# A ring of five raw slots, seven in the expert stage, with five high and four low split slots, and ScalarE's order around small turns

## Reference

```python
def swiglu(h, w_gate, w_up, w_down):
    return (jax.nn.silu(h @ w_gate) * (h @ w_up)) @ w_down

def moe_swiglu(h, w_router, b_router, w1, w3, w2):      # shortened
    top_val, top_idx = lax.top_k((xt @ w_router + b_router), 2)
    gates = jax.nn.softmax(top_val, axis=-1)
    ...                                                 # rows sorted by expert, in blocks
    def run_block(args):
        tok, e = args
        xb = x_pad[tok]
        hb = jax.nn.silu(xb @ w1[e]) * (xb @ w3[e])
        return hb @ w2[e]
    ...                                                 # each row times its gate, added to its token

def reference(x, c, ...):
    for l in range(2):
        sh_m, sc_m, g_m, sh_f, sc_f, g_f = split(silu(c) @ ada_w[l] + ada_b[l])
        h = rms_norm(x, norm_mix_pre[l]) * (1 + sc_m) + sh_m
        x = x + g_m * rms_norm(hybrid_mixer(h, ...), norm_mix_post[l])
        h = rms_norm(x, norm_ffn_pre[l]) * (1 + sc_f) + sh_f
        y = swiglu(h, ...) if l == 0 else moe_swiglu(h, ...)
        x = x + g_f * rms_norm(y, norm_ffn_post[l])
```

## Time and profile before

| | |
|---|---|
| time, median of 3 | 1459.69 us (1458.56 to 1461.4) |
| profiled execution | 1459.97 us; its span 1458.2 us |
| granted TensorE clock | 0.997 |
| PE busy | 1427.9 us, 98% |
| VectorE busy | 1278.9 us, 88% |
| ScalarE busy | 1022.2 us, 70% |
| moved by DMA | 506.88 MB, mean 348 GB/s |

### The profile page before, as it was taken

How to read it: one execution, slowest core, us unless ns; L and a number is a source line. 1 busy time by engine, 2 the same in 40 slices (tenths; PEclk the granted TensorE clock), 3 DMA queues, 4 the chain that set the end, 5 groups by cost and what they waited for, 6 DMA issues and landing times.

```text
span 1458.2 us, 18907 instructions
## 1 busy us (share of the span) xinstructions
PE 1427.9 (98%) x7352; PEld 1205.8 (83%) x7352; DVE 1278.9 (88%) x1263; ACT 1022.2 (70%) x992; POOL 81.5 (6%) x109
## 2 busy tenths in 40 slices
PE   9999999999999999999999999999999999999996
PEld 5799889878889988888888878788788788888885
DVE  6899888977777768999999989999998999999995
ACT  2774454434576358778888889888879888888874
POOL 5000000000000000000000002000000010000010
PEclk9999999999999999999999999999999999999998
DMA  9849859987554855999999999999999999999993
GB/s 371 342 181 355 311 180 387 388 346 268 184 195 145 287 219 211 374 414 367 406 422 421 420 377 399 409 421 420 418 418 408 409 414 420 420 409 420 421 409 116
DMA packets 74274, 506.88 MB, mean 348 GB/s; under 512 B 8385, under 2 KB 8513, under 8 KB 16706
## 3 DMA queue, kind: packets, MB, share of 16 engines
q1 hardware_dynamic: 69986, 490.91, 83.9%
q0 software_dynamic: 4192, 14.70, 3.4%
HBM read 498.74 MB, written 6.83 MB: 347 GB/s over the span
## 4 chain that ended last, share of the span: by engine, by line
PE 63%; issue 18%; DVE 14%; ACT 3%; DMA 1%; POOL 1%; SPq 0%; DVEq 0%; ACTq 0%; POOLq 0%
PE ps L1936 17%; PE ps L1938 16%; PE ps L1937 16%; DVE lo L1237 10%; PE ps L1997 2%; PE ps L2424 2%; PE ps L2425 2%; PE ps L2461 2%; ACT hi L698 2%; DMA gate_m<-rows_x,gather_row 1%; PE ps L2161 1%; PE ps L2144 1%; ACT hi L682 1%; DVE lo L1208 1%; DVE bT_lo L1767 1%
## 5 line engine op out<-in xcount | busy, mean ns | idle before, releaser
L1237 DVE TENSOR_TENSOR lo<-raw,hi 128x2048 fp32r<-128x2048 f32 x336 | 755.8, 2286 | 48.9 <-ACT hi L698 47.7
L698 ACT ACTIVATE hi<-raw 128x2048 fp32r<-128x2048 f32 x336 | 637.6, 1920 | 86.2 <-PE ps L1938 60.4
L1936 PE MATMUL ps<-hi,hT_hi 128*128 128x512 f32 (+3 forms) x896 | 348.2, 389 | 4.1 <-DVE hT_lo L1264 1.9
L1938 PE MATMUL ps<-hi,hT_lo 128*128 128x512 f32 (+3 forms) x896 | 342.5, 382 | 0.0
L1937 PE MATMUL ps<-lo,hT_hi 128*128 128x512 f32 (+3 forms) x896 | 342.2, 382 | 0.0
L1208 DVE TENSOR_TENSOR lo<-raw,hi 128x2048 fp32r<-128x2048 f32 (+3 forms) x83 | 176.9, 2145 | 37.6 <-ACT hi L682 36.2
L1936 PEld LDWEIGHTS ps<-hi,hT_hi 128*128 128x128 f32 x896 | 168.3, 188 | 38.7 <-issue 4.3
L1938 PEld LDWEIGHTS ps<-hi,hT_lo 128*128 128x128 f32 x896 | 168.2, 188 | 32.0
L1937 PEld LDWEIGHTS ps<-lo,hT_hi 128*128 128x128 f32 x896 | 168.4, 188 | 30.0 <-issue 0.2
L682 ACT ACTIVATE hi<-raw 128x2048 fp32r<-128x2048 f32 (+3 forms) x83 | 147.2, 1798 | 34.3 <-DMA raw<-in_w_fg_dram 15.2
L1936 PE MATMUL ps<-hi,bT_hi 128*128 128x512 f32 (+1 forms) x408 | 160.5, 393 | 7.2 <-DVE bT_lo L1767 7.1
(11 more groups left out here) (348 smaller groups left out, 1638.1 us busy)
## 6 DMA issues: line engine op xcount, KB each, us to landing
raw<-in_moe_w_dram SPq DMA_DIRECT2D x336, 1024.0 KB, 8.9
raw<-in_w_ada_dram SPq DMA_DIRECT2D x40, 1024.0 KB, 6.4
raw<-in_w_fd_dram SPq DMA_DIRECT2D x11, 1024.0 KB, 7.1
raw<-in_w_ga_dram SPq DMA_DIRECT2D x8, 1024.0 KB, 5.6
raw<-in_w_gb_dram SPq DMA_DIRECT2D x8, 1024.0 KB, 5.2
raw<-in_w_ab_dram SPq DMA_DIRECT2D x8, 1024.0 KB, 5.1
raw<-in_w_o_dram SPq DMA_DIRECT2D x8, 1024.0 KB, 6.9
raw<-in_w_fg_dram SPq DMA_DIRECT2D x8, 1024.0 KB, 6.7
```

The source lines that it names most:

```text
L698: act.activation(hi[:, (s - PLAIN) % NSPLIT, :], raw[:, r % NRAW, :], ACT.Copy).then_inc(hi_done, 1)
L1237: dve.tensor_tensor(lo[:, at, :], raw[:, r % NRAW, :], hi[:, at, :].bitcast(f32), ALU.subtract).then_inc(raw_done, 1)
L1936: pe.matmul(o, wh, mh, start=first, stop=False)
L1938: return pe.matmul(o, wl, mh, start=False, stop=last)
```

## The change

- `NSPLIT` = 4 becomes five `hi` slots (`NHIGH`) and four `lo` slots (`NLOW`). VectorE's `lo` now waits itself for `used` of the chunk four before; ScalarE's `hi` for the one five before.
- `NRAW` goes from 6 to 5. `raw_ring` works out for each load its slot and the load that had it before. From expert chunk 5 (`JOIN`) to chunk 319 (`LEAVE` is 320) two more slots are in the ring, both in r6. Their first loads wait for the zero rows (`rows_out`) and the normed rows (`xn_out`) to be written out.
- Small items' weighted rows go to `gate_m` instead of r6. For that a gather into `gate_m` waits for the scatter before it, and `weighted_y` of a small item for the turn of the next small item's rows. The last load of the result into r6 waits for the last chunk in the slot there.
- After a small unit, ScalarE makes `hi` of b+4 and b+5 first, then `small_silu`, then the silu or copy of w1, then `small_hi`.

The diff, cut to its core (elsewhere `raw[:, r % NRAW, ...]`, `hi[...]` and `lo[...]` are replaced by the helpers shown):

```diff
@@ -51,7 +51,9 @@
 SPARE = 3
 ITEMS = EXPERTS + SPARE
 CH = 2048
-NRAW, NSPLIT = 6, 4
+NRAW, NHIGH, NLOW = 5, 5, 4
+EXTRA = 2
+JOIN, LEAVE = 5, 320
 PER_ITEM = 6 * NG
 EPS = 1e-6
 NEG = -1.0e30
@@ -145,6 +147,29 @@
 STREAM = stream()
 RAW_OF = {(kind, n, q): r for r, (kind, n, q) in enumerate(STREAM)}
 NR = len(STREAM)
+
+
+def raw_ring():
+
+    out, free, fills, last = [], list(range(NRAW)), [0] * (NRAW + EXTRA), [None] * (NRAW + EXTRA)
+    for r in range(NR + ITEMS * PER_ITEM):
+        c = r - NR
+        if c == JOIN:
+            free = list(range(NRAW, NRAW + EXTRA)) + free
+        slot = free.pop(0)
+        if not (slot >= NRAW and c >= LEAVE):
+            free.append(slot)
+        else:
+            slot = free.pop(0)
+            free.append(slot)
+        fills[slot] += 1
+        out.append((slot, fills[slot], last[slot]))
+        last[slot] = r
+    return out
+
+
+RING = raw_ring()
+LAST_IN = [max(r for r, (s, _, _) in enumerate(RING) if s == slot) for slot in range(NRAW + EXTRA)]
 
 
 GATES = [(l, v) for l, v in ADA if v in (G_M, G_F)]
@@ -254,8 +279,8 @@
 
 
         raw = sb("raw", [P, NRAW, CH])
-        hi = sb("hi", [P, NSPLIT, CH], f32r)
-        lo = sb("lo", [P, NSPLIT, CH], f32r)
+        hi = sb("hi", [P, NHIGH, CH], f32r)
+        lo = sb("lo", [P, NLOW, CH], f32r)
         x = sb("x_tok", [P, T, D])
         r2 = sb("r2", [P, T * D])
         r3 = sb("r3", [P, T * D])
@@ -350,7 +375,7 @@
         x_rows_of = {False: cbc, True: gate_m}
         x_staged = {False: r3[:, 0:K * P].rearrange("p (k s) -> p k s", k=K),
                     True: r3[:, 1536:1536 + K * HALF_CAP].rearrange("p (k s) -> p k s", k=K)}
-        y_rows = {False: r5[:, :], True: r6[:, 0:D]}
+        y_rows = {False: r5[:, :], True: gate_m[:, :]}
 
         def x_pair(i):
 
@@ -368,6 +393,19 @@
         def large_slots(n):
             return slice(4, 8) if n == UNITS_ALL - 1 else slice(0, 4)
 
+        def raw_of(r, e=CH):
+            slot = RING[r][0]
+            return raw[:, slot, 0:e] if slot < NRAW else r6[:, (slot - NRAW) * CH:(slot - NRAW) * CH + e]
+
+        def high_of(s, e=CH):
+            return hi[:, (s - PLAIN) % NHIGH, 0:e]
+
+        def low_of(s, e=CH):
+            return lo[:, (s - PLAIN) % NLOW, 0:e]
+
+        def wait_full(engine, r):
+            engine.wait_ge(raw_full[RING[r][0]], 16 * RING[r][1])
+
         def h_at(m):
             return 4 + 8 * (m - 1) if m else 0
 
@@ -448,7 +486,13 @@
 
             def slot_free(r):
 
-                sp.wait_ge(raw_done, r + 1)
+                slot, fill, before_ = RING[r]
+                if before_ is not None:
+                    sp.wait_ge(raw_done, before_ + 1)
+                elif slot == NRAW:
+                    sp.wait_ge(rows_out, 16)
+                elif slot == NRAW + 1:
+                    sp.wait_ge(xn_out, 16)
 
             def early_load(s):
                 _, t, (a, b), _ = WEIGHTS[s]
@@ -478,16 +521,16 @@
                 else:
                     _, t, (a, b), e = WEIGHTS[n]
                     src = A[t][a, b]
-                sp.dma_start(raw[:, r % NRAW, 0:e], src).then_inc(raw_full[r % NRAW], 16)
+                sp.dma_start(raw_of(r, e), src).then_inc(raw_full[RING[r][0]], 16)
                 if kind == "first":
                     early_load(q)
 
             def moe_load(r, kind, e, g, half):
-                slot_free(r - NRAW)
+                slot_free(r)
                 src = A["moe_" + kind]
                 src = src[e, g, half] if isinstance(e, int) else \
                     src[bass.ds(e, 1), g, half, :, :].rearrange("e p n -> p (e n)")
-                sp.dma_start(raw[:, r % NRAW, :], src).then_inc(raw_full[r % NRAW], 16)
+                sp.dma_start(raw_of(r), src).then_inc(raw_full[RING[r][0]], 16)
 
             expert = {0: 0}
 
@@ -666,6 +711,7 @@
                 if n in FINISH_AT:
                     scatter_rows(FINISH_AT[n])
             pool.wait_ge(rows_out, ALL_ROWS)
+            pool.wait_ge(raw_done, LAST_IN[NRAW] + 1)
             pool.dma_start(y_exp, rows_y[0:SEQ].rearrange("(t p) d -> p t d", p=P)).then_inc(y_in, 16)
 
 
@@ -676,10 +722,10 @@
             def hi_part(s):
                 r = RAW_OF["w", s, 0]
                 e = WEIGHTS[s][3]
-                act.wait_ge(raw_full[r % NRAW], 16 * (r // NRAW + 1))
-                if s >= PLAIN + NSPLIT:
-                    act.wait_ge(used, s - NSPLIT + 1)
-                act.activation(hi[:, (s - PLAIN) % NSPLIT, 0:e], raw[:, r % NRAW, 0:e], ACT.Copy).then_inc(hi_done, 1)
+                wait_full(act, r)
+                if s >= PLAIN + NHIGH:
+                    act.wait_ge(used, s - NHIGH + 1)
+                act.activation(high_of(s, e), raw_of(r, e), ACT.Copy).then_inc(hi_done, 1)
 
             def upto(name, ahead=2):
 
@@ -1009,7 +1055,10 @@
 
                 small, before_ = i >= LARGE, same_kind_before(FINISH, i)
                 act.wait_ge(used, NW + unit_chunk(FINAL[i], "w2", 1) + 1)
-                act.wait_ge(rows_out, 16 if before_ is None else ROWS_OUT[before_])
+                if before_ is not None:
+                    act.wait_ge(rows_out, ROWS_OUT[before_])
+                if small and i + 1 < EXPERTS:
+                    act.wait_ge(m_gath, 2 * PREP_OF[i + 1] + 2)
                 bank = 6 if small else 4
                 act.activation(y_rows[small].rearrange("p (c s) -> p c s", c=2), ps[:, bank:bank + 2, :], ACT.Identity,
                                scale=held[:, i, 2:3]).then_inc(m_yc, 1)
@@ -1025,18 +1074,21 @@
                 if n in FINISH_AT:
                     weighted_y(FINISH_AT[n])
                 moe_hi(b + 3)
-                if n:
+                if n and SMALL[n - 1]:
+                    moe_hi(b + 4, b + 5)
+                    small_silu(n - 1)
+                elif n:
                     moe_hi(b + 4)
-                    (small_silu if SMALL[n - 1] else hidden_hi)(n - 1)
+                    hidden_hi(n - 1)
                     moe_hi(b + 5)
-                    if SMALL[n - 1]:
-                        small_hi(n - 1)
                 after = b + 6 if n else 4
                 up_done(n, "w1")
                 if SMALL[n]:
                     act.activation(gate_s, ps[:, 0, :], ACT.Copy).then_inc(m_silu, 1)
                 else:
                     act.activation(h_large, ps[:, 0, :], ACT.Silu).then_inc(m_silu, 1)
+                if n and SMALL[n - 1]:
+                    small_hi(n - 1)
                 if (i, g) == (END, 3):
                     act.wait_ge(m_gt, 1)
                     act.activation(r4[:, 512:512 + SEQ], ps[:, 3, 0:SEQ], ACT.Copy).then_inc(m_gtc, 1)
@@ -1141,9 +1193,9 @@
 
                 l, v = ADA[a]
                 r = RAW_OF["ada", a, q]
-                dve.wait_ge(raw_full[r % NRAW], 16 * (r // NRAW + 1))
+                wait_full(dve, r)
                 for kk in range(2):
-                    w = raw[:, r % NRAW, kk * D:(kk + 1) * D]
+                    w = raw_of(r)[:, kk * D:(kk + 1) * D]
                     k = 2 * q + kk
                     m = dve.scalar_tensor_tensor(w, w, 1.0, cbc[:, :], ALU.mult, ALU.mult, accum_out=av[:, k:k + 1])
                 m.then_inc(raw_done, 1)
@@ -1940,7 +1991,7 @@
             def chunk(name):
                 s = CHUNK[name]
                 pe.wait_ge(raw_done, RAW_OF["w", s, 0] + 1)
-                return hi[:, (s - PLAIN) % NSPLIT, :], lo[:, (s - PLAIN) % NSPLIT, :]
+                return high_of(s), low_of(s)
 
             def finish(name, m):
                 m.then_inc(used, 1)
```

More of the change, by code:

```diff
@@ L390, in build @@
         x_rooted = sem("x_rooted")
-        raw_full = [sem(f"raw_full{i}") for i in range(NRAW)]
+        raw_full = [sem(f"raw_full{i}") for i in range(NRAW + EXTRA)]
         early_in = [sem(f"early_in{s}") for s in range(PLAIN)]
@@ L463, in _ @@
             for r, (kind, n, q) in enumerate(STREAM):
-                if r >= NRAW:
-                    slot_free(r - NRAW)
+                slot_free(r)
                 if kind == "first" and q < 2:
@@ L649, in gather_rows @@
                     pool.wait_ge(m_gath, 2 * PREP_OF[before_] + 2)
+                if i >= LARGE and PREP_OF[i] > 4:
+                    pool.wait_ge(rows_out, ROWS_OUT[before_ - 1])
                 pool.indirect_dma_start(out=x_rows_of[i >= LARGE][:, :], out_offset=None, in_=rows_x,
@@ L695, in moe_hi @@
                     r, s = NR + c, NW + c
-                    act.wait_ge(raw_full[r % NRAW], 16 * (r // NRAW + 1))
-                    act.wait_ge(used, s - NSPLIT + 1)
-                    act.activation(hi[:, (s - PLAIN) % NSPLIT, :], raw[:, r % NRAW, :], ACT.Copy).then_inc(hi_done, 1)
+                    wait_full(act, r)
+                    act.wait_ge(used, s - NHIGH + 1)
+                    act.activation(high_of(s), raw_of(r), ACT.Copy).then_inc(hi_done, 1)
             def item_hi(i, lo_c, hi_c):
@@ L1206, in lo_part @@
                 dve.wait_ge(hi_done, s - PLAIN + 1)
```

(11 more changed lines are left out.)

## The result

The changed kernel takes 1452.38 us in the median of 5 runs (1452.11 to 1453.09), the kernel before 1459.69; the ratio is 0.9948, 95% interval 0.9936 to 0.996. On a second occasion it took 1452.85 beside 1460.85, ratio 0.9946 (0.9932 to 0.996). So it is faster, by 7.3 and 8.0 us, that is 0.5%, where 1452.5 was forecast.

What follows compares the result with a forecast made beforehand. PE, busy 98%, was taken to lose about 16 us in the expert stage, mainly to late DMA; 2.49 + 2.49 + 0.8 + 0.7 + 0.5 = 7.0, taken as 7.2, from 1459.97, less 0.3, gave 1452.5 us, range 1443.5 to 1461.5.

Steps and rivals of the forecast that it cites:

- No cost before the experts: Dense FFN (205 to 345 us) and mixers: five raw slots instead of six cost 0, between -1 and +5 us.
- The arithmetic of the ring: Dense FFN, 205 to 345 us: five slots allow 14.0 us from issue to release; a cycle needs 11.1, at most 13.1.
- One landing for the lead, -2.49 at the first small units: Expert stage, first small units: a seventh raw slot lets DMA be one chunk further ahead, -2.49 us.
- -2.49 and -0.8 for the hungry stretch from 841 us: Expert stage, 841 to 901 us: DMA slowed because six slots were full; the seventh wins 2.49, then 0.8 us.
- Who is late: DMA is: Expert stage: DMA, at share 1.01 and 421 GB/s in 701 to 841 us, is what PE waits for.
- The fifth high slot lets the order work: Small turns: with it `hi(b+5)` waits for the unit's first w1 chunk, not the second; 1.38 us per turn on VectorE go.
- Rival A: Expert stage: VectorE's bubbles, not DMA, set the pace; all 16 us of stalls go, 1444 us; chance 0.12.
- Rival B: Expert stage from 690 us: DMA is the ceiling, slots change little; -2.5 to 0, 1457.2 to 1459.7 us; chance 0.23.
- Rival C: Before the experts, 205 to 345 us and mixers: five slots pass 14.0 us and bind; slower, 1467 us; chance 0.15.

## Why the prediction was right, and where it was not

The time was forecast within 0.2 us, its sign and its range were right. The sum behind it was less right than its total, and that the total came out so close is in part luck. Of the sum, 2.49 + 2.49 + 0.8 + 0.7 = 6.5 us lie before 901 us; the changed kernel gains 3.7 us in the experts until there, and 3.3 on the second occasion. From 931 to 1166 us, for which the sum has next to nothing, it gains 3.8 in both, and then loses 1.4 and 1.0. And of the medians' 7.3 and 8.0 us the expert stage shows only 6.2 and 6.1.

*No cost before the experts*: right. PE is busy for all of 205 to 345 us with five raw slots, and from 60 to 560 us the lead over before stays between 1.61 and 1.69 us. ScalarE's waits for landings of w_fg grew, within PE's cover, from 15.2 to 26.2 us. The arithmetic of the ring (14.0 us allowed, 11.1 to 13.1 needed) held; used on five slots in the experts (12.6 allowed, 12.2 to 16.0 needed) it says that they bind, though not how much they cost, which was 16 us. The start was said to stay; the 1.6 us there are the execution's, not the change's.

*One landing for the lead, -2.49 at the first small units*: not so in place, nearly so in size. Until 841 us the changed kernel gains 1.6 us in the experts, and the one with six raw slots 1.4. The seventh slot is worth about 3 us, but only in the new order, and over the whole stage. With the old order it and the fifth high slot together gave 2.0.

*-2.49 and -0.8 for the hungry stretch from 841 us*: the wrong cause. The prediction laid it to six raw slots being full; with seven and the old order the rate is 358 GB/s still, with six, five high slots and the new order 407. Full slots say that someone frees them late, and I took their number for the reason. Late is ScalarE, which starts on a chunk 4.0 us after its landing there.

*"Who is late: DMA is"*: true of the changed kernel, not of the one before. The share of 1.01 was real, but with an eighth of the bytes gone the kernel before gained 2.8 us of the 18 that it loses and kept each stall on `bT_lo`. Two limits lay side by side. The chain that I read in the earlier trace rows, ScalarE's bubble, VectorE's bubble, PE's stall, made those 16 stalls, and it should have had a sum of its own.

*The fifth high slot lets the order work*: right, and shown by its absence in two kernels: both keep the 16 stalls on `bT_lo`.

*Rival A, all stalls go, 1444*: no. Removing VectorE's bubbles makes late transfers the limit after some 7 us; the changed kernel with fewer bytes, 1446.2, is where that rival ends when transfers are no limit. *Rival B*: its sign came, with ScalarE's waits for landings from 24.0 to 59.5 us, but its time did not. *Rival C*: no, in the stretch it named.

*Sizes.* A late matmul was put at its idle time plus 0.16 us; the following start is late too, by 0.08, so each of some 30 stalls costs about 0.24 beyond its idle time, and the stage lost about 18 us, not 16. The bubbles removed were to take 27 us off VectorE's waits for `hi`, to 20 or less; 12 went, and 32.9 are left. Landings are not the main reason, since with fewer bytes ScalarE waits 2.4 us for them and VectorE still 28.8 for `hi`. The prediction left out the large turns, for which ScalarE now waits 48.1 us instead of 15.3 with the next `hi` behind it; how much of the 32.9 is theirs, no run here shows. PE's idle time was to be 4 to 6 us; it is 7.7. DMA was to reach about 420 GB/s in 841 to 861 us; it reached 409. A landing was to take about 11 us, 2.49 more than before at most; it takes 3.0 to 3.2 more. And seven slots are not seven transfers in flight: 421 GB/s over 11.9 us are 4.8 chunks under way, where 8.9 us made 3.6, and the other slots hold chunks that wait for ScalarE or VectorE or are being worked on.

## What to carry to other kernels

A ring of slots has a cycle: slots x time per load must exceed landing + every step until release. Compute it for each stage: where five slots just met the median (12.6 us against 12.2), the sixth was worth 12.5 us and the seventh about 3. And find which step makes the cycle long. Where ScalarE came late to landed chunks, a seventh slot alone made the cycle longer (17.8 to 20.7 us) and left the rate as it was.

A wait that an engine takes in its list ahead of independent work can be moved behind that work only if the work's own target has a free slot; else the wait changes its name and nothing else. Order and slots are one edit. Look then at the next wait of the same kind: here ScalarE's waits for turns went from the small ones to the large ones.

Where DMA shows a share of 1 and PE shows stalls on another engine, take an eighth of the bytes away (for a measurement only, since the results are wrong): the stalls that stay are not DMA's.

## What was not expected of the hardware

TensorE's full clock comes at 10.0 us in one execution and at 16.4 in another, with the same matmuls ahead of it, and executions lie up to 1.6 us apart at 58 us. The page's row of granted clock does not show it; the distance between the starts of PE's matmuls does, 0.213 us against 0.112. A comparison by two profiles of effects below 2 us has to look at that first.

Behind a stall of 4.3 us PE was granted 0.69 of its clock in the next 5 us. In the kernel with eight raw slots three such stalls, 12.6 us of idle time, cost 5 us of clock on top.

With a seventh slot the landing grew from 8.9 us to 12, by more than the one transfer of 2.49 us that was allowed for, at the same 421 GB/s.
